# A six-layer network on one core: attention units of 128 queries of one head in place of 64 queries of two heads

## The chip, the cores and the metric

The kernel runs as one program on 1 core of one Trainium2 chip. The metric is the device time of one execution in microseconds (us). The core has five engines with an instruction queue each: TensorE (PE; its weight loads are listed apart, as PEld), VectorE (DVE), ScalarE (ACT), GpSimd (POOL) and SyncE (SP, which issues DMAs). Products read SBUF and write PSUM.

## The reference, cut to what matters

All in fp32, batch 1, 512 tokens of width 1024, heads 64 wide except where said. Two layers with four kinds of attention are followed by four layers of a second network; projections, norms, rotations, MLPs, a convolution and a Fourier mixer lie between them and are not touched. The attention parts:

```python
# layer ab: indexer-selected keys (DSA), 8 heads, and a band with sinks, 8 heads
p = masked_softmax(s, valid); o = einsum('bqgrk,bqkgd->bqgrd', p, vs)
m = maximum(max(s), sink); p = exp(s - m); p = p / (sum(p) + exp(sink - m))
...
# layer cd: NSA, 8 heads: compressed keys, selected blocks, window, each with a gate
o = gb[..., 0:1] * o_c + gb[..., 1:2] * o_s + gb[..., 2:3] * o_w
# and latent attention (MLA), 8 heads of 96 rows, causal
...
# grouped-query layer: 16 heads, 512 queries over 256 context + 512 latent keys; 256 context queries over 256
s = einsum('bqkgd,bnkd->bkgqn', q, k); p = softmax(s); o = einsum('bkgqn,bnkd->bqkgd', p, v)
...
# neighbourhood layer: 16 heads, 512 queries, a relative-position bias added to the latent keys' scores
s = concatenate([s_nb + bias, s_ctx]); p = softmax(s); o = p_nb @ v_nb + p_ctx @ v_ctx
```

## The kernel before

The whole network is a list of **stages**. Each engine walks the list; a gate (a semaphore per engine) keeps an engine from a stage until what it needs of the stages ahead is done. Five stages are attention; the text calls them A to E:

- **A** (291 to 381 us of the profiled execution): four passes of DSA, then four of the band with sinks.
- **B** (709 to 825 us): NSA, four times the passes compressed (31 keys), selected, window.
- **C** (976 to 1025 us): MLA, four passes. Heads have 96 rows here, so a unit is already 128 queries of one head.
- **D** (1304 to 1535 us): the grouped-query layer, eight passes of 512 queries over 768 keys, then eight context passes of 256 queries over 256 keys (from 1494 us on).
- **E** (2608 to 2804 us): neighbourhood attention, eight passes over 768 keys, with bias.

A **pass** handles two heads (64 rows each of the 128 partitions); a **unit** is 128 rows of the softmax. Before, a unit is 64 queries of both heads: its queries stand block-diagonally in a 128x128 tile, head 0 in the upper left, head 1 in the lower right, zeros elsewhere, so that one product over all 128 rows gives both heads' scores. GpSimd builds these tiles (`q_diagonal`, which lies in the buffer `sd`, four of them): two copies per unit, L2215 and L2216, the second of which releases TensorE by `q_ready`. A pass over 512 queries has eight units, a context pass four. C (`split=False`) doesn't use them.

For unit u the work goes round the engines:

1. TensorE, `scores(u)`: the product with up to 512 keys, for 768 keys two (512 and 256), L1188; then masks are added by bf16 products with a selection of the identity (`half_select`), L1192. It waits for `exp_done` of unit u-nb, whose score buffer in PSUM it reuses.
2. VectorE, `negmax(u)`: in E adds the bias to 512 of the scores (L1933), then reduces to minus the row's maximum (L1937; with a sink or a clamp L1940 and the small L1943).
3. ScalarE: the exponential into the SBUF buffer `probs`, with the row's sum (L1522, followed by a record ACTIVATION_READ_ACCUMULATOR, which carries `exp_done`); in the band also that of the sink (L1520).
4. VectorE, `scale(u)`: reciprocal of the sum (L1959), and the scaling of `probs` (L1965, with a gate L1963).
5. TensorE, `turn(u)`: transposes of 128x128 into one of nt transpose buffers, L1206. It waits for `probs_ready` and for `copied` of unit u-nt.
6. ScalarE, `copy_turned(u)`: PSUM to SBUF, L1505.
7. TensorE, `weigh`: V products of 64 output columns per head, on column halves of the array, L1225. Four units make a chunk of 256 queries; its products are issued in four quarters, one per turn of the loop. For 768 keys these are 2 or 4 products.
8. VectorE, `take`: the finished output of a pass.

The order on each engine is written out by a loop over u, with depths by the stage's largest key count:

```python
if st["keys_max"] <= BANK:                                   # stages A, B, C
    return dict(nb=4, wide=BANK, nt=2, scale=1, turn=3)
return dict(nb=2, wide=2 * BANK, nt=1, scale=1, turn=2)      # stages D, E
...
if u < U: scores(u)                                          # TensorE
if u >= lag + 4: weigh((u - lag - 4) // 4, (u - lag) % 4)
if lag <= u < U + lag: turn(u - lag)
...
if u >= lag: copy_turned(u - lag)                            # ScalarE, ahead of exp(u)
...
if u < U: negmax(u)                                          # VectorE
if d["scale"] <= u < U + d["scale"]: scale(u - d["scale"])
```

In E GpSimd also issues the loads of the bias, L2125: two DMAs per pass (64 partitions of 960 words, 240 KB) into one half of `CX` (two passes' buffers), the first two passes' at the stage's start, then one pass's every pass. The stage B gates are per query and head; `GH`, their order for units of two heads, is made in the compression stage ahead of B by four small products and a copy on ScalarE. The sinks are one input tile, loaded at the start of the program.

## Time and profile before

| | before |
|---|---|
| time, median of 3 runs (lowest, highest) | 4568.91 us (4565.99, 4574.04) |
| the profiled execution's own time | 4567.9 us |
| its span | 4566.1 us |
| TensorE busy, matmuls / weight loads | 4269.1 us (93%) / 2637.9 us (58%) |
| VectorE busy | 1795.3 us (39%) |
| ScalarE busy | 1001.0 us (22%) |
| GpSimd busy | 571.9 us (13%) |
| scores of all attention stages, L1188 | 315.5 us, 896 products |
| transposes, L1206 | 211.0 us, 1240 |

The span runs from the first instruction to the last; the rest of the time, 1.8 us, lies around it. Busy shares are over the whole program: a matmul counts as busy from its start to its modelled end, and weight loads run beside matmuls. The 40 slices of the page show TensorE at 90% or more in most of the program, with shares below that in some slices of its first third. In the rows below, the number behind "x" in a group is the count of instructions, "[1.42 <-PE psum L1206]" that the instruction's engine had been idle 1.42 us, ended by that instruction of TensorE, and PEclk the granted clock of TensorE as a part of 2.4 GHz.

### The profile page before, as it was taken

The numbers are of one execution on the slowest core, as the hardware profiler recorded it, in microseconds if no ns is written. First come the engines' busy times: TensorE is split into PE (matmuls) and PEld (weight loads), VectorE is DVE, ScalarE is ACT, GpSimd is POOL, SyncE is SP. The second block draws the span as 40 slices with busy tenths as digits, with TensorE's granted clock in tenths as the row PEclk, the third lists the DMA queues.
The fourth block names the chain that finished last, engine by engine and source line by source line (L and its number), as shares of the span: only waits on it lengthen the run. The fifth ranks groups of instructions, "written<-read, shape, count | busy, mean of one in ns | idle before, by whom it ended". The sixth has DMA issues, their size and how long they took to land. (4 is left out here: it accounts for less than half of the span.)

```text
span 4566.1 us, 41185 instructions
## 1 busy us (share of the span) xinstructions
PE 4269.1 (93%) x15852; PEld 2637.9 (58%) x15856; DVE 1795.3 (39%) x3063; ACT 1001.0 (22%) x2178; POOL 571.9 (13%) x896
## 2 busy tenths in 40 slices
PE   7998989799999799999989999999999999999998
PEld 3434454234545356656555455788644688746887
DVE  4355337552055321111010084566255565404343
ACT  1133015331135311110010153202123211112120
POOL 0021004110011100000000021211130111201112
PEclk8979978779979799999999999999999999999999
DMA  3211330201100112233111100344220344212221
GB/s 114 74 37 62 134 95 1 84 1 68 55 6 1 35 37 93 92 111 111 60 51 56 64 22 23 129 166 166 74 74 0 111 166 166 97 37 74 93 93 37
DMA packets 206735, 339.13 MB, mean 74 GB/s; under 512 B 19472, under 2 KB 77232, under 8 KB 206512
## 3 DMA queue, kind: packets, MB, share of 16 engines
q1 hardware_dynamic: 188000, 320.42, 20.2%
q10 hardware_dynamic: 17136, 10.07, 0.9%
q0 software_dynamic: 1408, 6.03, 0.5%
q8 instruction: 128, 2.10, 0.2%
q14 instruction: 63, 0.52, 0.0%
HBM read 330.48 MB, written 6.03 MB: 74 GB/s over the span
## 5 line engine op out<-in xcount | busy, mean ns | idle before, releaser
L1021 PE MATMUL psum<-H,ring 128*128 128x512 f32 (+1 forms) x2608 | 1140.1, 598 | 32.7 <-issue 17.0
L1021 PEld LDWEIGHTS psum<-H,ring 128*128 128x128 f32 (+1 forms) x2608 | 497.1, 191 | 658.5 <-issue 650.0
L1087 PE MATMUL psum<-arena,ring 128*128 128x256 f32 x1536 | 343.3, 380 | 2.8 <-ACT arena L1423 2.8
L1188 PE MATMUL psum<-arena,sd 128*128 128x256 f32 (+4 forms) x896 | 315.5, 459 | 14.8 <-POOL sd L2216 11.9
L1775 DVE SCALAR_TENSOR_TENSOR arena<-ring,cond,arena 128x512 f32<-128x512 f32 x448 | 319.0, 750 | 8.0
L1087 PEld LDWEIGHTS psum<-arena,ring 128*128 128x128 f32 x1536 | 290.4, 190 | 44.0 <-ACT arena L1423 5.2
L2151 POOL TENSOR_TENSOR ring<-ring 128x1024 f32<-128x1024 f32 x48 | 162.4, 3384 | 813.0 <-DVE arena L1665 813.0
L1087 PE MATMUL psum<-arena 128*128 128x256 f32 x1152 | 255.5, 379 | 0.0
L1937 DVE TENSOR_REDUCE small<-psum 128x1 f32<-128x768 f32 (+4 forms) x288 | 198.6, 690 | 126.2 <-PE psum L1188 79.5
L1505 ACT ACTIVATE arena<-psum 128x768 f32<-128x768 f32 (+5 forms) x352 | 191.5, 544 | 221.3 <-PE psum L1206 217.9
L1087 PEld LDWEIGHTS psum<-arena 128*128 128x128 f32 x1152 | 218.9, 190 | 29.8
L1758 DVE TENSOR_TENSOR mods<-psum,vec 128x4 f32<-128x4 f32 (+1 forms) x48 | 7.8, 162 | 563.8 <-PE psum L990 562.9
L1043 PE MATMUL psum<-arena,ring 128*128 128x512 f32 x512 | 225.4, 593 | 0.2 <-issue 0.2
L1522 ACT ACTIVATE arena<-psum,small 128x768 f32<-128x768 f32 (+5 forms) x352 | 219.4, 623 | 27.0 <-DVE small L1937 21.2
L1206 PE MATMUL psum<-ident,arena 128*128 128x128 f32 (+1 forms) x1240 | 211.0, 287 | 7.3 <-ACT arena L1505 3.2
L1021 PE MATMUL psum<-CH,ring 128*128 128x256 f32 x928 | 203.9, 379 | 0.0
L1188 PEld LDWEIGHTS psum<-arena,sd 128*128 128x128 f32 x896 | 153.5, 201 | 86.8 <-issue 79.1
L1206 PEld LDWEIGHTS psum<-ident,arena 128*128 128x128 f32 (+1 forms) x1240 | 133.7, 141 | 118.0 <-issue 80.9
L1225 PE MATMUL psum<-arena 128*64 128x256 f32 (+2 forms) x1360 | 192.5, 381 | 8.1 <-ACT arena L1505 7.1
L1021 PEld LDWEIGHTS psum<-CH,ring 128*128 128x128 f32 x928 | 176.3, 190 | 33.4 <-issue 10.5
L1087 PE MATMUL psum<-H,ring 128*128 128x256 f32 x768 | 183.2, 394 | 7.6 <-ACT H L1463 5.1
L1385 ACT ACTIVATE arena<-psum 128x512 f32<-128x512 f32 (+4 forms) x123 | 66.5, 542 | 510.7 <-PE psum L1021 510.4
(213 smaller groups left out, 4945.4 us busy)
## 6 DMA issues: line engine op xcount, KB each, us to landing
ring<-in_mlp_w SPq DMA_DIRECT2D x64, 2048.0 KB, 7.8
ring<-in_ada_w SPq DMA_DIRECT2D x48, 2048.0 KB, 7.9
ring<-in_na_qkv SPq DMA_DIRECT2D x6, 2048.0 KB, 8.0
ring<-in_pw SPq DMA_DIRECT2D x6, 2048.0 KB, 8.0
ring<-in_ab_in SPq DMA_DIRECT2D x5, 2048.0 KB, 7.8
ring<-in_cd_in SPq DMA_DIRECT2D x4, 2048.0 KB, 7.7
ring<-in_at_qkv SPq DMA_DIRECT2D x3, 2048.0 KB, 7.8
ring<-in_ab_out SPq DMA_DIRECT2D x2, 2048.0 KB, 10.3
```

What stands on the lines that cost most here:

```text
L1021: last = nc.tensor.matmul(out, lhs, rhs, start=(k == 0), stop=(k == len(t.pairs) - 1))
L1043: last = nc.tensor.matmul(bank(m), w[:, k, P * m:P * m + P], hid[:, KD * kb + k, :], start=(kb == 0 and k == 0), stop=(kb == 3 and k == KD ...
L1087: last = nc.tensor.matmul(out, w[:, i, P * m:P * m + P], x[:, i, :], start=(opens and m == 0 and i == 0), stop=(i == k - 1), skip_group_ch ...
L1188: last = nc.tensor.matmul(psum[:, buf + c0:buf + c1], q, p["k"](head, a * P + c0, a * P + c1), start=True, stop=not masks)
L1206: last = nc.tensor.transpose(psum[0:w, t0 + j * P:t0 + j * P + P], probs[u % d["nb"]][:, j * P:j * P + w], ident[:, :])
L1225: last = nc.tensor.matmul(psum[HD * g:HD * g + HD, (6 + pr % 2) * BANK + q0:(6 + pr % 2) * BANK + q1], p["v"](g, kt), turned_b[0:p["krows" ...
L1385: nc.scalar.activation(t.dst, src, ACT.Copy).then_inc(act_took, 1)
L1505: nc.scalar.activation(dst, src, ACT.Copy).then_inc(copied, 1)
L1522: nc.scalar.activation(probs[u % d["nb"]][:, 0:nk], psum[:, s0:s0 + nk], ACT.Exp, bias=small[:, c:c + 1], accum_out=small[:, 8 + c:9 + c]) ...
L1775: ins = nc.vector.scalar_tensor_tensor(partial[:, v, :], w[:, k, :], cond[:, k, v:v + 1], partial[:, v, :], ALU.mult, ALU.add)
L1937: nc.vector.tensor_reduce(small[:, c:c + 1], psum[:, s0:s0 + nk], AX, ALU.max, negate=True).then_inc(negmax_ready, 1)
L2151: nc.gpsimd.tensor_tensor(a21, a11, a21, ALU.subtract).then_inc(s3_made, 1)
```

## The change

A unit is now 128 queries of one head: unit j of a pass is head j mod 2 of query tile j div 2. A pass has as many units as before, over as many keys each. Nothing is built in advance: the queries of a head are its 64 rows of the projection, taken where they are (`of_head`). Scores are issued for two units at a time, at even u, chunk by chunk, head 0 on rows 0 to 63 and head 1 on rows 64 to 127 (in C one after the other, on 96 rows each). The masks keep their number and are added with the whole identity. `half_select`, `q_diagonal`, `q_ready` and the 640 copies on GpSimd are gone, as are the products and the copy that made `GH`.

The order changes on three engines. On TensorE transposes come before V products. On VectorE `negmax` is called for two units at even u, and `scale(u)` in turn u itself rather than one turn later. On ScalarE the copy stays ahead of the exponential in A, B and C, and comes behind it in D and E. `probs` has three buffers in D and E for two (the work area grows from 7680 to 8448 words per partition). The copies out of the transpose buffers write 128 queries of one head.

The sinks are loaded once for either head, onto both halves of the partitions (four DMAs for one, N_INPUTS 13 for 10). The bias lies in `CX` and `CH`, one for each of two passes, for each head on both halves of the partitions, the lower half one grid row on: four DMAs of 240 KB per pass for two. A pass's load waits for the last addition of the pass two before it.

```diff
@@ queries of one head on its 64 rows; sinks of both heads; NSA gates by unit
-                lambda g, q0, q1, t=t: QA[:, t, q0:q1], lambda g, k0, k1: KA[:, 0, k0:k1],
+                lambda g, q0, q1, t=t: of_head(QA[:, t, q0:q1], g), lambda g, k0, k1: of_head(KA[:, 0, k0:k1], g),
...
-                sink=sinks[:, t:t + 1]))
+                sink=lambda g, t=t: sinks[:, g, t:t + 1]))
...
-                gate=lambda j, t=t: GH[:, j % 2, j // 2, 3 * t:3 * t + 1]))
+                gate=lambda j, t=t: GC[:, j // 2, 12 * (j % 2) + 3 * t:12 * (j % 2) + 3 * t + 1]))
...
+        def of_head(x, g):
+            return x[HD * g:HD * g + HD]
@@ neighbourhood attention: two bias buffers
-        bias_buf = CX.rearrange("p t s -> p (t s)").rearrange("p (b n) -> p b n", b=2)
+        bias_buf = [x.rearrange("p t s -> p (t s)").rearrange("p (g n) -> p g n", g=2) for x in (CX, CH)]
@@ buffers and order
-            nb = 4 if km <= BANK else 2
+            nb = 4 if km <= BANK else 3
...
-                return dict(nb=4, wide=BANK, nt=2, scale=1, turn=3)
-            return dict(nb=2, wide=2 * BANK, nt=1, scale=1, turn=2)
+                return dict(nb=4, probs=4, wide=BANK, nt=2, turn=3, copy_first=True)
+            return dict(nb=2, probs=3, wide=2 * BANK, nt=1, turn=2, copy_first=False)
...
-            if p["split"]:
-                return None, HD * j, HD * j + HD
             return j % 2, P * (j // 2), P * (j // 2) + P
@@ TensorE
-                    if u >= d["nb"]:
-                        pe.wait_ge(exp_done, base + u - d["nb"] + 1)
-                    if head is None:
-                        pe.wait_ge(q_ready, n["split"] + 1)
...
+                    if u + 1 >= d["nb"]:
+                        pe.wait_ge(exp_done, base + u - d["nb"] + 2)
                     for c0 in range(0, nk, BANK):
                         c1 = min(nk, c0 + BANK)
-                        q = p["q"](head, q0, q1) if head is not None else q_diagonal[:, u % Q_BUFS, :]
-                        last = nc.tensor.matmul(psum[:, buf + c0:buf + c1], q, p["k"](head, a * P + c0, a * P + c1),
-                                                start=True, stop=not masks)
...
+                        for g in range(2):
+                            buf = ((u + g) % d["nb"]) * d["wide"]
+                            last = nc.tensor.matmul(psum[:, buf + c0:buf + c1], p["q"](g, q0, q1),
+                                                    p["k"](g, a * P + c0, a * P + c1), start=True, stop=not masks)
+                            if not masks and c1 == nk:
+                                last.then_inc(scores_ready, 1)
...
-                    if u < U:
+                    if u < U and u % 2 == 0:
                         scores(u)
+                    if lag <= u < U + lag:
+                        turn(u - lag)
                     if u >= lag + 4:
                         weigh((u - lag - 4) // 4, (u - lag) % 4)
-                    if lag <= u < U + lag:
-                        turn(u - lag)
@@ the compression stage loses the product and the copy that made GH
-                for half in range(2):
-                    for g in range(2):
-                        last = nc.tensor.matmul(bank(6)[HD * g:HD * g + HD, half * 12 * ST:(half + 1) * 12 * ST],
...
@@ ScalarE
-                    if u >= lag:
+                    if u >= lag and d["copy_first"]:
                         copy_turned(u - lag)
...
-                        if u >= d["nb"]:
-                            act.wait_ge(turned, base + u - d["nb"] + 1)
+                        if u >= d["probs"]:
+                            act.wait_ge(turned, base + u - d["probs"] + 1)
...
+                    if u >= lag and not d["copy_first"]:
+                        copy_turned(u - lag)
@@ VectorE
                         if j == 0:
-                            dve.wait_ge(bias_in[pi % 2], 32 * (pi // 2 + 1))
+                            dve.wait_ge(bias_in[pi % 2], 64 * (pi // 2 + 1))
...
+                    if u < U and u % 2 == 0:
+                        negmax(u)
+                        negmax(u + 1)
                     if u < U:
-                        negmax(u)
-                    if d["scale"] <= u < U + d["scale"]:
-                        scale(u - d["scale"])
+                        scale(u)
@@ GpSimd
                 for g in range(2):
-                    pool.dma_start(bias_buf[HD * g:HD * g + HD, t % 2, 0:15 * GRID],
-                                   rpb_table[2 * t + g].rearrange("c r j -> c (r j)")).then_inc(bias_in[t % 2], 16)
+                    for odd in range(2):
+                        pool.dma_start(bias_buf[t % 2][HD * odd:HD * odd + HD, g, GRID * odd:(15 + odd) * GRID],
+                                       rpb_table[2 * t + g].rearrange("c r j -> c (r j)")).then_inc(bias_in[t % 2], 16)
...
-                        nc.gpsimd.tensor_copy(q_diagonal[0:HD, u % Q_BUFS, 0:HD], q[0:HD]).then_inc(pool_steps, 1)
-                        nc.gpsimd.tensor_copy(q_diagonal[HD:P, u % Q_BUFS, HD:P], q[HD:P]).then_inc(q_ready, 1)
```

TensorE in the middle of stage D, before: `scores` (L1188) of one unit, then V products (L1225), then transposes (L1206).

```order
L1188 MATMUL psum<-arena,sd 128x512 [waits q_ready,exp_done]
L1188 MATMUL psum<-arena,sd 128x256
L1225 MATMUL psum<-arena 64x256 x4
L1206 MATMUL psum<-ident,arena 128x128 [waits copied,probs_ready]
L1206 MATMUL psum<-ident,arena 128x128 x5
L1188 MATMUL psum<-arena,sd 128x512 [waits q_ready,exp_done]
L1188 MATMUL psum<-arena,sd 128x256
L1225 MATMUL psum<-arena 64x256 x2
```

The same place after (scores are L1184, transposes L1206, V products L1225):

```order
L1184 MATMUL psum<-arena 128x512 [waits exp_done]
L1184 MATMUL psum<-arena 128x512
L1184 MATMUL psum<-arena 128x256 x2
L1206 MATMUL psum<-ident,arena 128x128 [waits copied,probs_ready]
L1206 MATMUL psum<-ident,arena 128x128 x5
L1225 MATMUL psum<-arena 64x256 x2
L1206 MATMUL psum<-ident,arena 128x128 [waits copied,probs_ready]
L1206 MATMUL psum<-ident,arena 128x128 x5
L1225 MATMUL psum<-arena 64x256 x4
```

Two units' scores moved to one place, with the wait for the second unit's score buffer ahead of both, and both units' transposes and V products lie between two such places.

ScalarE at the start of stage D, before: exponentials (L1522) and copies (L1505).

```order
L1522 ACTIVATE arena,small<-psum,small 128x768 [waits negmax_ready] x2
L1505 ACTIVATE arena<-psum 128x12x64 [waits turned]
L1522 ACTIVATE arena,small<-psum,small 128x768 [waits turned,negmax_ready]
L1505 ACTIVATE arena<-psum 128x12x64 [waits turned]
L1522 ACTIVATE arena,small<-psum,small 128x768 [waits turned,negmax_ready]
```

After (exponentials L1512, copies L1495):

```order
L1512 ACTIVATE arena,small<-psum,small 128x768 [waits negmax_ready] x3
L1495 ACTIVATE arena<-psum 128x6x128 [waits turned]
L1512 ACTIVATE arena,small<-psum,small 128x768 [waits turned,negmax_ready]
L1495 ACTIVATE arena<-psum 128x6x128 [waits turned]
L1512 ACTIVATE arena,small<-psum,small 128x768 [waits turned,negmax_ready]
```

The copy of unit u-2 moved behind the exponential of unit u.

VectorE at the start of stage D, before: reduction (L1937), reciprocal (L1959), scaling (L1965).

```order
L1937 TENSOR_REDUCE small<-psum 128x1 [waits scores_ready]
L1959 RECIPROCAL small<-small 128x1 [waits exp_done]
L1965 TENSOR_SCALAR arena<-arena,small 128x768 [waits dve_steps]
L1937 TENSOR_REDUCE small<-psum 128x1 [waits scores_ready]
L1959 RECIPROCAL small<-small 128x1 [waits exp_done]
L1965 TENSOR_SCALAR arena<-arena,small 128x768 [waits dve_steps]
```

After (L1923, L1945, L1951):

```order
L1923 TENSOR_REDUCE small<-psum 128x1 [waits scores_ready] x2
L1945 RECIPROCAL small<-small 128x1 [waits exp_done]
L1951 TENSOR_SCALAR arena<-arena,small 128x768 [waits dve_steps]
L1945 RECIPROCAL small<-small 128x1 [waits exp_done]
```

Two reductions moved together, ahead of both units' scalings, of which the first needs the exponential of the unit reduced just before.

## Rows read from the trace of the kernel before

**Rows 1.** Busy us (instructions) of PE, PEld, DVE, ACT, POOL; PEclk, DMA share, GB/s.

```profile
291.00:381.00 90.00, 85.31 (x556) 51.00 (x560) 69.91 (x264) 62.27 (x226) 31.51 (x127) 0.97 0.01 1
...
1304.00:1470.00 166.00, 165.35 (x882) 93.26 (x883) 98.41 (x178) 96.33 (x172) 28.86 (x124) 0.98 0.02 4
...
2608.00:2804.00 196.00, 189.72 (x1024) 107.12 (x1024) 154.35 (x264) 108.75 (x192) 36.25 (x139) 0.98 0.10 27
```

**Rows 2.** The same view: one pass of stage D, one of stage E.

```profile
1332.50:1355.70 23.20, 23.20 (x130) 13.05 (x129) 13.80 (x27) 13.55 (x24) 3.75 (x16) 1.00 0.00 1
...
2640.00:2663.20 23.20, 23.20 (x130) 13.07 (x129) 19.20 (x33) 13.58 (x26) 4.78 (x18) 1.00 0.09 22
```

**Rows 3.** Timeline of stage D: start us, us, engine, line, operation, out<-in, form, count.

```profile
1402.29 1.46 PE L1188 MATMUL psum<-arena,sd 128*128 128x512 f32 x4
...
1403.20 0.90 ACT L1522 ACTIVATE arena<-psum,small 128x768 f32<-128x768 f32 x1
...
1403.68 1.08 PE L1225 MATMUL psum<-arena 128*64 128x256 f32 x8
1403.79 0.96 DVE L1937 TENSOR_REDUCE small<-psum 128x1 f32<-128x768 f32 x1 [1.00 <-PE psum L1188]
...
1403.98 0.20 ACT L1522 ACTIVATION_READ_ACCUMULATOR arena<-psum,small 128x1 f32 x1
...
1404.69 0.87 PE L1206 MATMUL psum<-ident,arena 128*128 128x128 f32 x6
...
1405.40 1.46 PE L1188 MATMUL psum<-arena,sd 128*128 128x512 f32 x4
...
1405.61 0.81 ACT L1505 ACTIVATE arena<-psum 128x768 f32<-128x768 f32 x1 [1.42 <-PE psum L1206]
```

**Rows 4.** Timeline of the compression stage: two products on opposite row halves.

```profile
645.64 1.06 PE L1262 MATMUL psum<-arena,ident 64*64 64x512 f32 x1
...
645.68 1.06 PE L1263 MATMUL psum<-arena,ident 64*64 64x512 f32 x1
```

**Rows 5.** Stage E: groups by shape, bias addition; timeline, its first instance.

```profile
L1933 DVE TENSOR_TENSOR psum<-psum,CX 128x512 f32<-128x512 f32 x64 | 44.7, 699 | 248.9 <-DMA CX<-rpb_table 224.1 <-PE psum L1188 24.8
...
2613.99 0.70 DVE L1933 TENSOR_TENSOR psum<-psum,CX 128x512 f32<-128x512 f32 x1 [224.11 <-DMA CX<-rpb_table]
```

**Rows 6.** Timeline of stage D's context passes (256 keys).

```profile
1502.67 0.44 PE L1206 MATMUL psum<-ident,arena 128*128 128x128 f32 x2
...
1502.95 0.60 PE L1188 MATMUL psum<-arena,sd 128*128 128x256 f32 x2
...
1504.12 0.38 ACT L1505 ACTIVATE arena<-psum 128x256 f32<-128x256 f32 x1
...
1504.40 0.47 ACT L1522 ACTIVATE arena<-psum,small 128x256 f32<-128x256 f32 x1
...
1504.67 0.65 PE L1225 MATMUL psum<-arena 128*64 128x256 f32 x4
...
1504.78 0.42 DVE L1937 TENSOR_REDUCE small<-psum 128x1 f32<-128x256 f32 x1 [0.21 <-PE psum L1188]
...
1505.25 0.44 PE L1206 MATMUL psum<-ident,arena 128*128 128x128 f32 x2
```

**Rows 7.** One line's instructions, stage A: ns min/median/max, first and last start.

```profile
L1522 ACT ACTIVATE arena<-psum,small x24: 359/522/692, 303.3 to 338.1; 128x128 f32<-128x128 f32 x6, 128x256 f32<-128x256 f32 x6, 128x384 f32<-128x384 f32 x6, 128x512 f32<-128x512 f32 x6
...
L1522 ACT ACTIVATE arena<-psum,small x24: 348/455/466, 339.1 to 368.4; 128x256 f32<-128x256 f32 x18, 128x128 f32<-128x128 f32 x6
...
L1520 ACT ACTIVATE small<-sinks,small x32: 285/294/301, 337.9 to 377.2; 128x1 f32<-128x1 f32 x32
```

**Rows 8.** The same view as rows 1: two stretches before stage D, one much later.

```profile
1289.90:1296.80 6.90, 4.11 (x16) 1.81 (x16) 3.31 (x5) 1.30 (x3) 0.00 (x0) 0.99 0.00 0
1296.80:1310.40 13.60, 11.40 (x21) 6.01 (x22) 4.53 (x9) 2.48 (x4) 3.29 (x14) 0.50 0.16 41
3488.00:3508.60 20.60, 14.24 (x32) 5.91 (x32) 8.06 (x9) 8.93 (x13) 0.00 (x0) 1.00 0.00 0
```

More of the change, by code:

```diff
@@ L348, in build_program @@
         top[0] = 0
-        WORK = 7680
+        WORK = 8448
         work = reserve(6144)
@@ L405, in attn_pass @@
         def attn_pass(q, k, v, keys, pv, dst=None, z=None, masks=None, first=True, last=True, n=S, gate=None, sink=None,
-                      clamp=False, bias=None, krows=P, split=True):
+                      clamp=False, bias=None, krows=P):
             return dict(q=q, k=k, v=v, keys=keys, pv=pv, dst=dst, z=z, masks=masks, first=first, last=last, n=n,
-                        units=2 * n // P, gate=gate, sink=sink, clamp=clamp, bias=bias, krows=krows, split=split)
+                        units=2 * n // P, gate=gate, sink=sink, clamp=clamp, bias=bias, krows=krows)
+        def of_head(x, g):
+            return x[HD * g:HD * g + HD]
         passes = []
@@ L722, in build_program @@
         top[0] = 0
-        work = reserve(7680)
+        work = reserve(WORK)
         QN = reserve(8 * S).rearrange("p (t s) -> p t s", s=S)
@@ L884, in build_program @@
             n_tab += 16 * len(st["loads"])
-        N_INPUTS = 10
+        N_INPUTS = 13
         sd_count = misc_count = 0
@@ L909, in _ @@
                              (arena[:, P:2 * P], dram["prev_mask"]),
-                             (sinks[:, :], dram["sinks"])):
+                             *((sinks[HD * half:HD * half + HD, g, :], dram["sinks"][HD * g:HD * g + HD])
+                               for half in range(2) for g in range(2))):
                 sp.dma_start(dst, src).then_inc(inputs_in, 16)
@@ L1285, in compress @@
                     last.then_inc(misc_pe, 1)
[L1286 to L1292 removed]
+                n["misc"] += 6
             def latnorm(st):
@@ L1498, in copy_turned @@
                     q0, q1 = q0 % CHUNK, (q1 - 1) % CHUNK + 1
-                    if p["split"]:
-                        src = psum[0:rows, t0:t0 + (b - a) * P].rearrange("p (t g s) -> p t g s", g=2, s=HD)
-                        dst = turned_b[0:rows, chunk % 2, a:b, :, q0:q1]
-                    else:
-                        src = psum[0:rows, t0:t0 + (b - a) * P].rearrange("p (t s) -> p t s", s=P)
-                        dst = turned_b[0:rows, chunk % 2, a:b, g, q0:q1]
+                    src = psum[0:rows, t0:t0 + (b - a) * P].rearrange("p (t s) -> p t s", s=P)
+                    dst = turned_b[0:rows, chunk % 2, a:b, g, q0:q1]
                     nc.scalar.activation(dst, src, ACT.Copy).then_inc(copied, 1)
@@ L1611, in _ @@
             step(nc.scalar.activation(identb[:, :], ident[:, :], ACT.Copy))
-            for half in range(2):
-                for g in range(2):
-                    step(nc.scalar.activation(half_select[:, half, HD * g:HD * g + HD], ident[:, HD * half:HD * half + HD],
-                                              ACT.Copy))
             step(nc.scalar.activation(diagm[:, :], arena[:, 0:P], ACT.Copy))
@@ L1940, in negmax @@
                     chain(nc.vector.tensor_reduce(small[:, 40 + c:41 + c], psum[:, s0:s0 + nk], AX, ALU.max))
-                    other = p["sink"] if p["sink"] is not None else -1e29
+                    other = p["sink"](j % 2) if p["sink"] is not None else -1e29
                     nc.vector.tensor_scalar(small[:, c:c + 1], small[:, 40 + c:41 + c], other, -1.0, ALU.max,
@@ L2118, in _ @@
         def _(pool):
-            n = dict(yn=0, rope=0, swap=0, unit=0, split=0)
+            n = dict(yn=0, rope=0, swap=0, unit=0)
             pool_count = n_downs = 0
@@ L2199, in _ @@
                         pool.wait_ge(cos_ready, n["swap"])
[L2200 to L2222 removed]
+                if st["kind"] == "attention" and st["passes"][0]["bias"] is not None:
+                    for t in range(len(st["passes"])):
+                        if t >= 2:
+                            pool.wait_ge(bias_used, t - 1)
+                        load_bias(t)
                 pool.sem_inc(stage_of["pool"], 1)
```

91 lines of the change are left out of this document (31 added, 60 removed).

## The prediction, before the changed kernel was run

> **What bounds the kernel now.** The page's first part has TensorE busy 93% of the span, but the change touches only the five attention stages, so the view to open is the busy time by stretch. [rows 1] gives three of the five, A, D and E (B and C read like A): in each TensorE is busy 95 to 100%, VectorE 59 to 79%, ScalarE 55 to 69%. Inside stages D and E one pass of eight units takes 23.20 us, all of it TensorE [rows 2]: 5.80 us for two units. So what a unit costs there is TensorE's work, and [rows 3] shows why nothing else shows: scores start at 1402.29, then V products (1403.68), then transposes (1404.69), then the next scores (1405.40), with no gap, while the reduction, the exponential and the copy of other units run beside them. The band passes of stage A are the exception: 24 exponentials in 29.3 us, 1.27 us a unit [rows 7], where ScalarE and VectorE have little slack left.
>
> **The rate that halves.** A unit's scores (512 and 256 keys) hold TensorE 1.46 us, 1.29 of it streaming, the rest the way out [rows 3]. Do two fp32 products on different halves of the array really run together? The trace has such a pair: L1262 and L1263, each on 64 rows and 64 columns, start 0.04 us apart and take 1.06 us each [rows 4]. I take it that the pair's scores take what one unit's take now, plus 0.04. Per pair TensorE's work then falls from 5.80 by 1.29 for the scores, and gains one more change of array shape (row-half scores, full-array transposes, column-half V products, twice round): about 0.10 to 0.20 each, by the start-to-start times around L1225 in [rows 3]. That would leave some 4.7 us per pair.
>
> **The loop that closes.** But the change also reorders. Before, scores(u+1) were ready while unit u was still being worked on, and copies came before exponentials. Now, in stages D and E, TensorE runs scores(u,u+1), transposes(u-2), V, transposes(u-1), V, and only then the next scores. Transposes(u-1) need the one transpose buffer that copy(u-2) frees; copy(u-2) stands behind exp(u) on ScalarE; exp(u) needs the reduction of scores(u). So one round is, all from [rows 3]: scores 1.46 + 0.04; hand-over 0.04 and reduction 0.96; hand-over 0.04 and exponential with its accumulator read 0.88 (0.78 to the read's start and 0.10 until the copy can start); copy 0.81 and hand-over 0.04; transposes 0.71 and a shape change 0.10; V products (the odd turn's eight records) 1.01 and a shape change 0.10. Sum 6.19 us per pair. The hand-over is the 0.04 between TensorE's end at 1403.75 and the reduction at 1403.79. Against 5.80: +0.39, over 32 pairs **+12**. The saved 1.29 us would be TensorE idle while it waits for that copy.
>
> Stage E has the bias addition in front of the reduction, 0.70 us [rows 5] and 0.03 until the next: 6.92 per pair, +1.12 over 32 pairs **+36**. Before, this addition was hidden behind TensorE; its cover is gone. Context passes (256 keys, 16 pairs) repeat every 2.58 us (transposes at 1502.67 and 1505.25) [rows 6]; the same loop there is scores 0.60 + 0.04, reduction 0.46, exponential 0.45, copy 0.38 + 0.04, transposes 0.28 + 0.10, V 0.58 + 0.10: 3.03, so +0.45 x 16 = **+7**.
>
> Stages A to C have four score buffers and two transpose buffers, so that loop is open. Another closes: VectorE now issues reduce(u), reduce(u+1), scale(u), scale(u+1), and no longer scales one unit behind. Scale(u+1) waits for exp(u), copy and exp(u+1). For a band pair: reduction 0.42 and its small operation 0.2; ScalarE twice 0.2 (sink, 0.29 long, overlapped) and 0.45, once 0.27 for the copy, the accumulator's tail 0.1; hand-overs 0.1; three small operations 0.37 and the scaling 0.27: 3.0 us, against 2 x 1.27 [rows 6, 7]: +0.45 x 16 = **+7**. In the four sparse-attention passes TensorE was the limit (24 units in 34.8 us, 1.51 each, so 3.0 per pair [rows 7]); the loop at their mean of 320 keys is 2.6, so they gain 0.3 x 16, of which the fill at the stage's start takes a part: **-4**. In stage B the passes with little TensorE work (31 keys, 20 gates) lose as the band does and the longer ones gain: **+7**, in C nothing is concurrent (96 rows), the fill alone costs **+2**; I keep both between -5 and +15.
>
> **Small edits.** The 640 GpSimd copies ran in TensorE's shadow; gone, they give back only the first wait of a stage, and there ScalarE's table load ends at the same time: -1 each in A and B, nothing in D, whose first reduction waits for a table. The lost gate copy: -1. Three more sink transfers ahead of the first gate: +1.5. Four bias transfers per pass for two: the first addition already waited for them until 2613.99 [rows 5], so +2.5. Together +1. The masks keep their number.
>
> **Sum:** 12+36+7+7-4+7+2+1 = +68 on the profiled execution's 4567.9 us, which lies 1.0 below the median: 4636 to 4637; **4637**.
>
> **Bounds of what the trace doesn't show.** A change into and out of row halves: nothing at all, or twice what the column halves cost, so 0.2 us less or more on the loop of 80 pairs: 16 us either way. Hand-overs through more semaphores, +-0.05 on four of them: another 10. This gives 4610 to 4665 for this case alone.
>
> **A rule of the skill against the sum.** The Trainium skill, TensorEngine Tiling (Array Packing), Theoretical Speedup, gives up to 2x for a contraction of 64 or less. Taken alone it speaks for a faster kernel, by the saving of the second rival below; [rows 4] agrees with the concurrency, and whether it reaches the span is what the loop decides.
>
> **Rivals.**
> *Clock.* Inside D and E the granted clock is 1.00, the 2.4 GHz level, with TensorE busy throughout [rows 2]. In my loop it idles 1.4 us of 6.2 in D and 2.1 of 6.9 in E. It fell to 0.50, 1.2 GHz, behind a stretch busy 4.1 of 6.9 us, and held 1.00 over one busy 14.2 of 20.6 [rows 8], which E's loop resembles. At 1.2 GHz the streams in the loop double: 1.29 + 0.65 + 0.86 = 2.8 us per pair; a third of D's and E's 64 pairs gives +60, all +180: 4700 to 4815. Chance 0.12, of which 0.05 below 4715.
> *Faster.* If the copy of u-2 finds its place before exp(u), or TensorE's waits overlap more than I count, TensorE stays the limit at 4.7 us per pair: -1.1 x 64, -5 for context and sparse passes, the band's +7 kept: about -70, **4498**. The mechanism is the transposes' wait; it decides once that wait is under 0.4 us of the 1.4 I give it in D. For it: [rows 1], where VectorE and ScalarE have 20 to 45% to spare. Against it: they are spare because they wait, and the order in which ScalarE issues is fixed. 0.11. This is also where the skill's figure of up to 2x for the scores would show in full.
> *No concurrency.* If the second head's scores follow the first's, the first chunk's other head adds 0.86 to 64 loops, and 8 in stages A and B: +63, 4700. [rows 4] speaks against. 0.05.
> *A draw:* both loops 1 us shorter in E, as if the bias were still hidden: about 4570 to 4595. 0.04, half of it within 0.2%.
>
> **How the numbers follow.** The forecast's case has 0.68. About 9 us (0.2%) is what a measurement of this kernel can tell from no change. Faster 0.11, same 0.02, slower 0.87. The case's own range is 4610 to 4665; the range given also takes in the draw's upper half, the rival without concurrency and the clock's lower part: 4580 to 4715. Outside are the faster case, 0.02 of the draw and 0.07 of the clock's, together 0.20.
>
> **What would show it.** Right: in D and E one idle stretch of TensorE per pair, before every second L1206, ended by ScalarE's copy; 24.8 us per pass in D, 27.7 in E; scores of a pair 1.5 us; stage A within 5 us of before; clock 1.00. Wrong: pass times under 23.2 us, L1206 never waiting, a clock of 0.5 inside D or E, or scores of a pair near 2.6 us.

## The result, and the profile after

The changed kernel takes 4685.88 us (median of 4 runs, 4672.25 to 4689.46) against 4568.07 for the kernel before: a ratio of 1.025, 95% interval 1.0227 to 1.0274. That is 118 us slower; forecast were 69 (4637, range 4580 to 4715). 4686 lies outside the forecast case's own range of 4610 to 4665; it lies inside the range given, through the part of the clock's rival that was added to it. The profiled execution took 4688.96 us, its span is 4687.2.

Busy time by stretch of the changed kernel, columns as in [rows 1]. The stretches are stages A and B, stage D over the same 166 us as there, one pass of D, its context passes, stage E, one pass of E, and a piece of stage B:

```profile
291.00:386.00 95.00, 80.42 (x556) 42.00 (x560) 72.28 (x263) 60.28 (x226) 0.00 (x0) 0.93 0.00 1
711.70:837.00 125.30, 116.27 (x704) 56.96 (x704) 93.10 (x355) 77.31 (x290) 0.00 (x0) 0.81 0.00 1
...
1317.50:1483.50 166.00, 124.89 (x802) 69.26 (x802) 93.19 (x165) 89.33 (x159) 0.00 (x0) 0.96 0.02 4
1350.00:1374.90 24.90, 19.01 (x130) 10.58 (x128) 14.16 (x25) 13.56 (x24) 0.00 (x0) 1.00 0.00 1
1516.00:1571.70 55.70, 39.18 (x248) 18.23 (x248) 32.39 (x107) 29.32 (x99) 0.00 (x0) 1.00 0.00 1
2643.10:2919.10 276.00, 191.04 (x1024) 102.17 (x1024) 154.18 (x264) 111.34 (x194) 16.92 (x32) 0.82 0.14 37
2700.00:2732.50 32.50, 23.68 (x126) 12.52 (x122) 18.78 (x33) 12.89 (x23) 2.10 (x4) 0.82 0.13 31
...
751.50:765.10 13.60, 13.53 (x51) 6.40 (x52) 9.30 (x29) 7.18 (x23) 0.00 (x0) 0.50 0.01 2
```

In the pass of D TensorE needs 19.01 us where it needed 23.20 [rows 2], so the scores did get cheaper, and the pass still takes 24.9: it idles for 5.9. In the pass of E it idles for 8.8, and the granted clock is 0.82 of full speed, so 1.2 GHz for part of the time; its 23.68 us busy therefore hold some work at half speed.

Where the 121 us of the span came from, by the start of the first product of each part in both traces (A to E are counted to the start of the weights or the stage that the line names):

| | before | after | difference | forecast |
|---|---|---|---|---|
| up to the first product of A | 291.4 | 291.1 | 0 | +1.5 |
| A, to the projection's second block | 121.4 | 125.6 | +4 | +2 |
| the compression stage and around | 296.8 | 295.1 | -2 | -1 |
| B, to the start of C | 266.7 | 278.7 | +12 | +6 |
| C and what follows it | 328.2 | 327.0 | -1 | +2 |
| D, to the next stage's weights | 282.1 | 307.0 | +25 | +19 |
| what lies between D and E | 1021.8 | 1018.6 | -3 | 0 |
| E, to the next stage's weights | 195.7 | 276.7 | +81 | +38.5 |
| from there to the end | 1762.0 | 1767.4 | +5 | 0 |

The last line is code that both kernels share, and the runs of the changed kernel differ by 17 us among themselves; I leave those 5 us unexplained. The 3 us between D and E have a reason that the forecast left out. Before, GpSimd issued the bias loads and then built the first tiles, and TensorE waited 4.39 us for them:

```profile
2604.02 0.37 SPq L923 DMA_DIRECT2D ring<-in_mlp_w  x1
...
2605.42 2.25 POOL L2125 DMA_DIRECT2D CX<-rpb_table  x4
...
2608.38 5.46 PE L1188 MATMUL psum<-arena,sd 128*128 128x512 f32 x8 [4.39 <-POOL sd L2216]
```

Now the first scores follow the projection after 0.80 us. E is the line to look into.

Timeline of stage D after, one pair of units, columns as in [rows 3]:

```profile
1400.32 0.88 PE L1206 MATMUL psum<-ident,arena 128*128 128x128 f32 x6
1400.42 1.82 DVE L1923 TENSOR_REDUCE small<-psum 128x1 f32<-128x768 f32 x2 [1.80 <-PE psum L1184]
1401.12 0.65 PE L1225 MATMUL psum<-arena 128*64 128x256 f32 x4
1401.41 0.90 ACT L1512 ACTIVATE arena<-psum,small 128x768 f32<-128x768 f32 x1 [2.69 <-DVE small L1923]
...
1402.30 0.80 ACT L1495 ACTIVATE arena<-psum 128x768 f32<-128x768 f32 x1
...
1402.63 0.62 DVE L1951 TENSOR_SCALAR arena<-arena,small 128x768 f32<-128x768 f32 x1
...
1403.25 0.85 PE L1206 MATMUL psum<-ident,arena 128*128 128x128 f32 x6 [1.47 <-DVE arena L1951]
...
1404.02 1.08 PE L1225 MATMUL psum<-arena 128*64 128x256 f32 x8
...
1405.04 1.56 PE L1184 MATMUL psum<-arena 64*128 64x512 f32 x8
1406.53 0.87 PE L1206 MATMUL psum<-ident,arena 128*128 128x128 f32 x6
1406.63 1.82 DVE L1923 TENSOR_REDUCE small<-psum 128x1 f32<-128x768 f32 x2 [1.79 <-PE psum L1184]
```

From one group of transposes to the same one a pair on: 1406.53 - 1400.32 = 6.21 us, forecast 6.19. The eight records of two units' scores take 1.56 us, about what one unit's four took (1.46, [rows 3]). The idle time stands ahead of the second transposes, as forecast. Its label needs care: it names the scaling L1951, whose end at 1403.25 is the very instant at which the transposes start. By the program that scaling is the next unit's, not theirs, and in the next piece, from E, it ends at 2755.85, 0.45 behind their start (2755.40). The copy L1495 ends at 1403.10, 0.15 before; in the piece from E the same wait stands 0.15 behind the same copy and is labelled so.

Timeline of stage E after, two pairs:

```profile
2751.74 0.87 PE L1206 MATMUL psum<-ident,arena 128*128 128x128 f32 x6
2751.84 0.70 DVE L1919 TENSOR_TENSOR psum<-psum,CH 128x512 f32<-128x512 f32 x1 [3.31 <-PE psum L1184]
...
2752.57 0.96 DVE L1923 TENSOR_REDUCE small<-psum 128x1 f32<-128x768 f32 x1
...
2753.56 0.90 ACT L1512 ACTIVATE arena<-psum,small 128x768 f32<-128x768 f32 x1 [5.05 <-DVE small L1923]
...
2754.45 0.80 ACT L1495 ACTIVATE arena<-psum 128x768 f32<-128x768 f32 x1
...
2755.23 0.62 DVE L1951 TENSOR_SCALAR arena<-arena,small 128x768 f32<-128x768 f32 x1
...
2755.40 1.51 PE L1206 MATMUL psum<-ident,arena 128*128 128x128 f32 x6 [2.21 <-ACT arena L1495]
...
2756.84 1.89 PE L1225 MATMUL psum<-arena 128*64 128x256 f32 x8
...
2760.15 0.87 PE L1206 MATMUL psum<-ident,arena 128*128 128x128 f32 x6
...
2763.82 0.84 PE L1206 MATMUL psum<-ident,arena 128*128 128x128 f32 x6 [2.21 <-ACT arena L1495]
...
2767.10 0.88 PE L1206 MATMUL psum<-ident,arena 128*128 128x128 f32 x6
```

The second pair takes 2767.10 - 2760.15 = 6.95 us, forecast 6.92. The first takes 8.41: its transposes (1.51 for 0.84) and V products (1.89 for 1.08) ran at the lower clock. So the round of E has the forecast length at 2.4 GHz, and over a pass of four pairs the clock adds 32.5 - 27.8 = 4.7 us (27.8 is four times 6.95).

### The profile page after: what moved, and what is told of

Same layout as the page of the kernel before. It is cut to its first block and busy times, and to the rows that moved or that the text cites. A ratio compares the mean times of both kernels' runs of the same rounds, so it can differ in the third digit from the quotient of the medians.

```text
span 4687.2 us, 40238 instructions
## 1 busy us (share of the span) xinstructions
PE 4237.6 (90%) x15844; PEld 2595.2 (55%) x15848; DVE 1805.0 (39%) x3063; ACT 995.3 (21%) x2173; POOL 422.0 (9%) x264
## 5 line engine op out<-in xcount | busy, mean ns | idle before, releaser
L1206 PE MATMUL psum<-ident,arena 128*128 128x128 f32 (+1 forms) x1240 | 221.2, 300 | 152.8 <-ACT arena L1495 86.0
L1512 ACT ACTIVATE arena<-psum,small 128x768 f32<-128x768 f32 (+5 forms) x352 | 220.9, 628 | 297.1 <-DVE small L1923 281.8
L1206 PEld LDWEIGHTS psum<-ident,arena 128*128 128x128 f32 (+1 forms) x1240 | 143.9, 149 | 244.8 <-issue 189.7
L1184 PE MATMUL psum<-arena 64*128 64x512 f32 (+4 forms) x960 | 224.9, 552 | 24.6 <-ACT arena L1512 18.4
L1923 DVE TENSOR_REDUCE small<-psum 128x1 f32<-128x768 f32 (+4 forms) x288 | 188.2, 686 | 82.5 <-PE psum L1184 72.2
L1225 PE MATMUL psum<-arena 128*64 128x256 f32 (+2 forms) x1360 | 207.9, 407 | 3.4 <-ACT arena L1495 2.7
L1495 ACT ACTIVATE arena<-psum 128x768 f32<-128x768 f32 (+5 forms) x352 | 190.5, 541 | 57.1 <-PE psum L1206 48.5
L1085 PE MATMUL psum<-CX,arena 128*128 128x256 f32 x768 | 173.3, 379 | 3.3 <-DVE CX L1671 3.3
```

The costliest lines, as they stand in the source:

```text
L1085: last = nc.tensor.matmul(out, w[:, i, P * m:P * m + P], x[:, i, :], start=(opens and m == 0 and i == 0), stop=(i == k - 1), skip_group_ch ...
L1184: last = nc.tensor.matmul(psum[:, buf + c0:buf + c1], p["q"](g, q0, q1), p["k"](g, a * P + c0, a * P + c1), start=True, stop=not masks)
L1206: last = nc.tensor.transpose(psum[0:w, t0 + j * P:t0 + j * P + P], probs[u % d["probs"]][:, j * P:j * P + w], ident[:, :])
L1225: last = nc.tensor.matmul(psum[HD * g:HD * g + HD, (6 + pr % 2) * BANK + q0:(6 + pr % 2) * BANK + q1], p["v"](g, kt), turned_b[0:p["krows" ...
L1495: nc.scalar.activation(dst, src, ACT.Copy).then_inc(copied, 1)
L1512: nc.scalar.activation(probs[u % d["probs"]][:, 0:nk], psum[:, s0:s0 + nk], ACT.Exp, bias=small[:, c:c + 1], accum_out=small[:, 8 + c:9 + ...
```

## The experiments

Each is an edit to the changed kernel, of 4685.88 us, or to the experiment named. Ratios are to the kernel before, measured beside them on the same chip (4568.6 to 4569.2 us).

### V products first again in D and E

```diff
-                    if lag <= u < U + lag:
+                    if lag <= u < U + lag and not d["weigh_first"]:
                         turn(u - lag)
                     if u >= lag + 4:
                         weigh((u - lag - 4) // 4, (u - lag) % 4)
+                    if lag <= u < U + lag and d["weigh_first"]:
+                        turn(u - lag)
```

> Edit to the changed kernel: in stages D and E TensorE issues the V products ahead of the transposes again, as before the change; nothing else. My theory: the round scores, reduction, exponential, copy(u-2), transposes(u-1), V, next scores is what sets a pair's time (6.2 us in D, 6.9 in E at full clock). With the V products in front, they run while VectorE reduces, and the next scores stand right behind the transposes: D falls from 248.8 us (first scores to last V product, 24.9 per pass) to about 215 (21 per pass), E from 264 to about 210 (25 per pass), and with less idle time the 1.2 GHz stretches in E vanish. Total about 4590. Rival, the copy behind the exponential is what counts and the place of the V products hardly matters: D stays over 24 us per pass, total over 4660. Rival, the score buffers' release by the second exponential bounds D too: D at 23 to 24, total 4620 to 4650.

Measured: 4589.95 us, ratio 1.0044 (1.0029 to 1.0059). A pass of D, a pass of E:

```profile
1340.00:1360.90 20.90, 19.06 (x130) 10.61 (x131) 13.69 (x25) 13.59 (x25) 0.00 (x0) 1.00 0.00 1
2660.00:2684.00 24.00, 19.12 (x128) 10.59 (x128) 19.33 (x35) 13.75 (x25) 2.14 (x5) 1.00 0.17 42
```

The same 19.1 us of TensorE work in passes of 20.9 and 24.0. The order of two steps on TensorE alone is worth 96 us, of which some 34 come through E's clock (see the fourth experiment); D is now shorter than before the change (23.2), E not (23.2). In E's passes behind the first the clock is 1.00. What holds them at 24.0 is a second round, which the first had hidden. The weight loads of the next pair's scores (PEld) start when the second exponential of the pair is done:

```profile
2661.17 0.30 PEld L1184 LDWEIGHTS psum<-arena 64*128 64x128 f32 x4 [0.31 <-ACT arena L1514]
...
2667.13 0.30 PEld L1184 LDWEIGHTS psum<-arena 64*128 64x128 f32 x4 [0.20 <-ACT arena L1514]
```

The exponential frees the score buffer, as the second rival of the expectation has it, though at a lower price: 5.96 us from scores to scores by way of addition, reduction, exponential, copy and second exponential, so 24 per pass. (The second unit's reduction ends in the same hundredths as the copy lets the exponential start, so VectorE's two additions and reductions would bring the same.) In D the same round lacks the addition and takes 5.2, so 20.9 per pass.

### Copy ahead of the exponential again in D and E

```diff
-            return dict(nb=2, probs=3, wide=2 * BANK, nt=1, turn=2, copy_first=False)
+            return dict(nb=2, probs=3, wide=2 * BANK, nt=1, turn=2, copy_first=True)
```

> Edit to the changed kernel: in stages D and E ScalarE copies unit u-2 ahead of the exponential of unit u, as before the change; TensorE's order stays as changed. My theory: transposes(u-1) no longer wait for the reduction and exponential of u, but the exponential of u waits for the copy of u-2 and so for its transposes; I expect D a little shorter (about 24 us per pass, 240 us), E much shorter (about 24.5 per pass, 205 us in place of 264), since the bias addition is hidden behind transposes and copy, and clock 1.00 in E. Total about 4615. Rival, that only the order on TensorE matters: no change, 4686 within 10.

Measured: 4616.59 us, ratio 1.0108 (1.0093 to 1.0123). The passes take 24.0 us in both stages, with clock 1.00:

```profile
1360.00:1384.00 24.00, 19.28 (x131) 10.62 (x130) 14.21 (x26) 13.55 (x24) 0.00 (x0) 1.00 0.00 1
2710.00:2734.00 24.00, 19.23 (x128) 10.59 (x128) 19.26 (x35) 13.78 (x24) 2.10 (x4) 1.00 0.17 42
```

That D and E are now equal says that the bias addition left the path: the round through reduction and exponential is open. (The 6.0 us per pair that are left are the scores, two groups of transposes with their copies, and the second exponential.) So the copy's place behind the exponential is one link of the forecast's round, the V products' place another, and either one cut opens it.

### E without the bias addition

```diff
-                        chain(nc.vector.tensor_tensor(psum[:, s0:s0 + S], psum[:, s0:s0 + S], p["bias"](j), ALU.add))
```

> Edit to the changed kernel: the bias addition of stage E is left out (the output lacks it there); its loads and their waits stay. My theory: the addition lies openly in the round, 0.70 us per pair at full clock, and by making TensorE idle longer it brings the stretches at 1.2 GHz. Without it E reads like D: 24.9 us per pass for 32.5, clock 1.00, total 4686 - 60 = about 4626. Rival, the slow clock comes from the late start of E (the wait for the bias) and would be there without the addition: 28 to 30 us per pass, total 4650 to 4665. Rival, the addition is hidden: 32 us per pass.

Measured: 4624.02 us, ratio 1.0125 (1.0108 to 1.0142). One pass of E:

```profile
2700.00:2724.90 24.90, 19.00 (x130) 10.58 (x128) 14.22 (x26) 13.56 (x24) 2.05 (x4) 1.00 0.16 40
```

This is D's pass (24.9 us, 19.0 of it busy), at clock 1.00. The addition stands once per pair in the round; at full clock it costs 27.8 - 24.9 = 2.9 us per pass (the 27.8 is in the next experiment), and 4.7 more through the clock.

### TensorE kept busy in E's gap

```diff
+                    if u % 2 and lag + 4 <= u < U + lag and st["passes"][0]["bias"] is not None:
+                        for _ in range(4):
+                            nc.tensor.matmul(bank(6 + pairs[0] % 2, CHUNK), zeros[:, :], X[:, 0, 0:CHUNK],
+                                             start=False, stop=False, skip_group_check=True)
                     if lag <= u < U + lag:
                         turn(u - lag)
```

> Edit to the changed kernel: in stage E, where TensorE stands idle for 2.2 us ahead of every second group of transposes, it first issues four products of 256 columns with a zero matrix, added to the output bank it already owns (1.7 us at full clock); they change nothing of the result. My theory: the idle time makes the granted clock fall to 0.50 for parts of E, and that costs the 4.8 us per pass over the 27.7 that the round gives. With the gap filled the clock stays at 1.00 and E takes 27.7 to 28.5 us per pass, total 4686 - 35 = about 4650, though TensorE has more to do. Rival, the round itself is longer than I add it up and the clock no more than a sign of that: 32.5 us per pass or more, total 4686 to 4720.

Measured: 4656.06 us, ratio 1.019 (1.0174 to 1.0205), that is 30 less than without the extra work (`zeros` is a new tile, set to 0 at the start). One pass of E:

```profile
2720.00:2747.80 27.80, 26.68 (x163) 16.37 (x162) 19.31 (x34) 13.71 (x24) 2.10 (x4) 1.00 0.15 36
```

TensorE does 26.7 us of work where the round's own takes 19.0 at full clock (row 2665.00 of the next experiment), and the pass is 4.7 us shorter: the clock is 1.00. From the first exponential of E to the last it is 218.5 us where the changed kernel takes 253.0, so the clock cost 34.5 us there. Filling the idle gap is thus enough to hold the clock. That the gap alone brings the fall isn't shown: in the next experiment two passes with the same gap held 1.00.

### VectorE's scaling one unit behind again in A, B and C

```diff
-                    if u < U:
-                        scale(u)
+                    if d["scale"] <= u < U + d["scale"]:
+                        scale(u - d["scale"])
```

(`scale=1` in A to C, 0 in D and E.)

> Edit to the changed kernel: in stages A, B and C VectorE scales unit u-1 after the two reductions, one unit behind, as before the change; D and E stay as changed. My theory: in these stages the round reduction, exponential, copy, second exponential, scaling, reduction sets the time of the band passes (12.3 us) and of the compressed ones (8.2), and the lag opens it: A from 86.8 us (first to last scores) to about 76, B from 118.6 to about 106, C unchanged; total 4686 - 23 = about 4663. Rival, the band passes are held by ScalarE's own work (three instructions per unit): A gains under 4 us, total over 4675.

Measured: 4655.99 us, ratio 1.0191 (1.0177 to 1.0205), 30 less for 23 expected. From the end of a stage's first exponential to the end of its last A takes 80.1 us (89.4 as changed, 84.8 before), B 105.6 (119.6, 109.9), C 43.9 (43.1, 42.4), together 22.5 less, as expected. Some 4 of B's 14 are its clock: as changed it had a stretch at 0.50 (751 to 765 us, above), and with the shorter passes it has none there; and the first four experiments leave B as it is, and B took 115 us in the two whose granted clock there was 0.91 and 0.92, 120 to 121 in the two at 0.81 and 0.80. The surplus over the sum is E's clock: from first exponential to last E takes 241.8 us for 253.0, though nothing in it changed. D's passes stay at 24.9. E's show again what the clock does: the same instructions take 27.8 us in one pass and 34.0 in another.

```profile
2665.00:2692.80 27.80, 18.96 (x128) 10.59 (x128) 18.79 (x33) 13.72 (x25) 2.10 (x4) 1.00 0.15 36
2720.00:2754.00 34.00, 25.17 (x128) 13.17 (x128) 19.29 (x34) 13.70 (x24) 2.10 (x4) 0.80 0.12 30
```

### Both heads' scores on the same half of the array

```diff
-                            last = nc.tensor.matmul(psum[:, buf + c0:buf + c1], p["q"](g, q0, q1),
-                                                    p["k"](g, a * P + c0, a * P + c1), start=True, stop=not masks)
+                            last = nc.tensor.matmul(psum[:, buf + c0:buf + c1], p["q"](0, q0, q1),
+                                                    p["k"](0, a * P + c0, a * P + c1), start=True, stop=not masks)
```

> Edit to the changed kernel: both heads' scores are computed from head 0's rows, so both on the upper half of the array (the second head's output is head 0's); everything else stays. My theory: scores of two heads on opposite halves run together, and a pair takes 1.56 us for what would be 2.8; since they stand in the round, doing without adds 0.86 us per pair of D and E before the first reduction can start (its other chunk adds to the second unit alone), 3.4 us per pass, and 4 us in each of A and B: total 4686 + 63 = about 4750. Rival, two heads' products don't run together, or the saved time lies wholly under the wait for the copy: 4686 within 15.

Measured: 4829.3 us (4808.36 to 4853.58), ratio 1.0573 (1.0532 to 1.0613). Timeline of D, and two stretches, one pass of D and 65 us of stage B:

```profile
1440.38 2.85 PE L1184 MATMUL psum<-arena 64*128 64x512 f32 x8
```

```profile
1440.00:1468.30 28.30, 24.11 (x132) 13.47 (x128) 13.56 (x25) 13.57 (x25) 0.00 (x0) 1.00 0.00 1
...
795.00:860.00 65.00, 65.00 (x217) 31.84 (x215) 30.36 (x106) 24.23 (x88) 0.00 (x0) 0.50 0.00 1
```

D did as expected: 28.3 us per pass, 3.4 more, and the pair's scores take 2.85 us on one half against 1.56 on two. So opposite halves do run together, 1.8 times as fast, and what remains of the gain lies in the round, not under its wait. The total missed by 80 us. The four runs lie in two groups, 4808 and 4810, 4849 and 4854, and the profiled one is the longest, with 165 us more span than the changed kernel's for 63 expected. Of the 102 that are over, 78 lie in A and B: from first exponential to last these take 118.6 and 176.4 us (89.4 and 119.6 as changed, +4 expected for each). The second row shows where: for 65 us TensorE was busy without a break at a granted 0.50. Another 16 lie in E, whose passes behind the first take 36.0 to 40.7 us at 0.66 to 0.81, and 6 in D's first pass. What in the products brings the low clock I didn't test; it is told again below.

### All together, and two steps more

The seventh kernel joins the first and fifth experiments, and issues the second pass's bias only when the first has landed:

```diff
                         if t >= 2:
                             pool.wait_ge(bias_used, t - 1)
+                        if t == 1:
+                            pool.wait_ge(bias_in[0], 64)
```

> Edit to the changed kernel: V products ahead of transposes in D and E (as the first experiment), VectorE's scaling one unit behind in A to C (as the fifth), and the second pass's bias is loaded in E only when the first pass's has landed. My theory: the effects add up: 4590 - 23 - 4 for the bias = about 4563, within 0.2% of the kernel before, D at 20.9 us per pass and 15 us shorter than before, E at 24.0 and some 8 us longer than before. Rival, effects overlap: 4575 to 4590.

Measured: 4565.48 us, ratio 0.9992 (0.9983 to 1.0001): no difference from before. The parts add up, but the bias gave nothing. The first addition stands 2596.32 - 2584.18 = 12.1 us behind the first scores, as it did with both passes' loads at once (12.6 as changed, 2655.71 - 2643.11; 11.4 in the first experiment):

```profile
2583.42 0.37 SPq L923 DMA_DIRECT2D ring<-in_mlp_w  x1
...
2584.18 1.56 PE L1184 MATMUL psum<-arena 64*128 64x512 f32 x8 [0.80 <-issue]
...
2584.69 2.25 POOL L2115 DMA_DIRECT2D CX<-rpb_table  x4 [239.46 <-ACTq L1621]
...
2596.32 0.70 DVE L1921 TENSOR_TENSOR psum<-psum,CX 128x512 f32<-128x512 f32 x1 [227.04 <-DMA CX<-rpb_table]
```

So it isn't the second pass's loads that hold the first's. The 2 MB weight load L923 had been issued 1.3 us ahead of it; that the bias stands behind that load is likely but not shown, since no run moved it. The eighth kernel sets the transposes four units behind the scores in A to C (`turn=4`):

> The seventh experiment's kernel, and in A to C the transposes come four units behind the scores instead of three. My theory: with four score buffers the pair at u then isn't held by transposes whose scaling has just been issued; A, B and C gain 2 to 7 us each, total 12 under the seventh: about 4551, faster than before by 0.3 to 0.4%. Rival, TensorE is full there already (its work per unit is the limit): no difference.

Measured: 4556.99 us, ratio 0.9974 (0.9964 to 0.9984). A takes 77.6 us from first exponential to last, B 99.6, C 41.7, together 10.7 less than in the seventh; the median fell by 8.5. The ninth loads the first pass's bias one stage earlier:

```diff
+                if s + 1 < len(stages) and stages[s + 1]["kind"] == "attention" and stages[s + 1]["passes"][0]["bias"] is not None:
+                    load_bias(0)
...
-                        if t == 1:
-                            pool.wait_ge(bias_in[0], 64)
-                        load_bias(t)
+                        if t:
+                            load_bias(t)
```

> The eighth experiment's kernel, with the first pass's bias loaded one stage earlier, while TensorE still makes queries, keys and values of stage E (CX is free then), the second pass's at E's start. My theory: E starts with 12 us in which VectorE waits for the bias and TensorE for VectorE, and then runs its first pass at 1.2 GHz for a part; with the bias there, the first addition stands right behind the first scores (about 1.7 us), and the first pass takes 25 us for 29: total 13 to 15 under the eighth, about 4543, that is 0.5% under the kernel before. Rival, the transfers only collide with the weight loads of the projection and hold TensorE there by as much: no difference, 4557 within 4.

Measured: 4545.6 us, ratio 0.9945 (0.9932 to 0.9959), 11.4 less for 13 to 15 expected. Timeline at E's start:

```profile
2571.03 1.56 PE L1184 MATMUL psum<-arena 64*128 64x512 f32 x8 [0.80 <-issue]
...
2572.79 0.70 DVE L1921 TENSOR_TENSOR psum<-psum,CX 128x512 f32<-128x512 f32 x1 [216.67 <-PE psum L1184]
```

The wait fell from 12.1 to 1.8 us; the first pass stayed at 28.3 us, where I had expected 25. This kernel beats both, by 23.6 us (0.55%) the one before. From first exponential to last D takes 12.7 us less than before and A and B together 19, while E, with passes of 24.0 for 23.2, takes 10.9 more. Not all of this is the change's: four units between scores and transposes in A to C could have been tried in the kernel before too, and weren't.

## Why the forecast was right, and where its sizes were off

*Scores at half the price:* right. 1.56 us for a pair against 1.46 for a unit, and 2.85 when both stand on one half. TensorE's work in a pass of D fell from 23.20 to 19.01 us, 4.75 per pair for the forecast's 4.7. The Trainium skill, TensorEngine Tiling (Array Packing), Theoretical Speedup, gives up to 2x here; the runs show 1.8 for the scores and, in the kernel as changed, less than nothing for the span.

*The loop that closes:* right, in place and size: 6.21 us per pair in D for 6.19, 6.95 in E at full clock for 6.92, 6.2 per context pass, so 3.1 per pair for 3.03. Cutting either of two links opened it (D's pass 20.9 and 24.0 us for 24.9), and taking out the addition made E's pass D's. D's total came out at +25 for 19; the passes gave +16 for 12, of which 4.6 in the first one, which runs partly at 0.50 while the stage fills (0.79 over the pass, 0.95 before). The bound for the hand-overs is too small by its own terms: four of 0.05 us in 80 pairs are 16 us, not 10; nothing hangs on it.

*The bias without its cover:* right, 2.9 us per pass at full clock, forecast 4 x 0.73.

*Stages A to C:* A right. The sparse passes together are 3.4 us shorter (forecast 4), the band passes 8.0 longer (7), and the lag on VectorE gave more than the band's loss back. B came out at +12 for +6, with its clock, C at -1 for +2.

*The clock as a rival with chance 0.12:* this is the step that failed. I set E's loop beside a stretch of the trace that had held 1.00 with the same busy share [rows 8], and took it for safe. E fell to 0.50 for part of every pass, which cost 4.5 to 6.1 us in each but the first and 34 in all; the fourth experiment gives them back by filling the gap, for 30 us in the median. Stage B lost another 4 or so at 0.50, and D's first pass its 4.6. The list of signs has "a clock of 0.5 inside D or E" among those of being wrong: that one was seen. That 4686 still lies in the range is owed to the rival's lower part, 0.05 of the chances, and not to the forecast's case. My mechanism for the clock and its price were there, only in the rival: a third of the pairs at 1.2 GHz, +60. It came out between that and nothing. The two cases did not exclude each other, and should have been one case with a term for the clock.

*The small edits:* nearly right, by an offset that the forecast didn't see. The first addition stood 12.6 us behind the scores, before 5.6 (2613.99 less 2608.38), 7 more for 2.5. But the scores themselves no longer wait 4.39 us for GpSimd's tiles, and counted from the issue of the weight load L923 the addition comes 13.4 us behind (2655.71 less 2642.34), before 10.0 (2613.99 less 2604.02): the bias loads cost 3.4 us. The rest, 3.6, is the earlier start of the scores, and stands in the table with the opposite sign, between D and E.

So of the 53 us by which the span's 121 exceeds the sum's 68, 34 are the clock in E, some 4 the clock in B and 4.6 D's first pass; the part behind E has 5 that stay unexplained, and the rest is the sum of small misses of both signs.

## What to carry to other kernels

Work taken from the busiest engine shows in the time only as far as no round through the other engines closes. Write the round out step by step in the new order of issue, with the buffers that tie it, before counting what was saved: here the 1.05 us of TensorE's work saved per pair in D went whole into a wait of 1.47, and swapping two steps in the engine's order of issue was worth 96 us. Where a change makes TensorE idle in every round, price each of its steps at both clock levels, and try the order that leaves no gap first. When a round is opened, look for the next one: here it was the release of the score buffers, which keeps E above its old length. A label of what ended a wait is only as good as the instants behind it: here the releaser named in D ended in the same hundredth as the wait, and the same scaling in E, 0.45 us too late, shows that it wasn't the one.

## What I had not expected of the hardware

The granted clock stayed at 0.50 while TensorE was busy without a break. It fell behind a stretch with gaps, and then stayed low over 13.53 us busy of 13.60 in the changed kernel (row 751.50) and over 65.00 of 65.00 in the sixth experiment (row 795.00, with the scores on 64 rows one behind the other). Four rows of stage B: as changed, ahead of the one; in the sixth experiment, ahead of the other; in the fifth experiment; before the change:

```profile
748.00:751.50 3.50, 2.51 (x20) 1.12 (x20) 2.77 (x16) 2.06 (x12) 0.00 (x0) 1.00 0.00 0
...
783.00:790.00 7.00, 6.40 (x47) 3.69 (x47) 5.75 (x35) 3.96 (x22) 0.00 (x0) 1.00 0.00 0
...
716.60:805.00 88.40, 84.83 (x598) 42.30 (x596) 73.88 (x291) 65.09 (x240) 0.00 (x0) 1.00 0.01 1
...
725.00:825.00 100.00, 95.95 (x643) 55.36 (x641) 79.46 (x299) 69.33 (x251) 40.56 (x156) 1.00 0.01 1
```

So in this kernel a full row of busy tenths didn't mean full speed. Half-row products alone don't settle it: the fifth experiment has the same scores in pairs as the changed kernel and held 1.00 over 88 us, and D in the sixth held 1.00 at 24.11 us busy of 28.30. Which property of the work decides stays open.

Also, the same instructions in the same order took 27.8 us in one pass of E and 34.0 in another of the same execution. Where the loop sits at the edge of the clock's fall, its time isn't one number: the runs of the changed kernel spread by 17 us, those before by 8.
